# RWKV layer: one masked copy for both heads' grams of a chunk, and the key rates multiplied on ScalarE

## The reference

```python
a = jax.nn.sigmoid(a0 + fa @ w_a2)
kk = (k * k_k).reshape(b, s, RWKV_HEADS, HEAD_DIM).astype(jnp.float32)
kk = kk / jnp.maximum(jnp.linalg.norm(kk, axis=-1, keepdims=True), L2_EPS)
k = k * (1 + (a - 1) * k_a)
def step(state, inp):
    r_t, w_t, k_t, v_t, kk_t, a_t = inp
    sa = jnp.einsum('bhij,bhj->bhi', state, -kk_t)
    state = (state * w_t[:, :, None, :]
             + sa[..., None] * (kk_t * a_t)[:, :, None, :]
             + v_t[..., None] * k_t[:, :, None, :])
    y_t = jnp.einsum('bhij,bhj->bhi', state, r_t)
    return state, y_t
```

## Time and profile before

| | us |
|---|---|
| median of 3 runs | 1768.92 |
| lowest and highest | 1768.81 and 1769.65 |
| the profiled execution, its time | 1768.42 |
| its span, first to last instruction | 1766.6 |

### The profile page before, as it was taken

One profiled execution on the slowest core, in us unless ns is written; L12 is line 12 of the kernel. 1 busy time (PEld: TensorE's weight loads), 2 busy tenths in 40 slices (PEclk: granted clock), 3 DMA queues, 4 the chain that ended last, 5 costly groups with the idle time before them and its releaser, 6 DMA issues.

```text
span 1766.6 us, 22241 instructions
## 1 busy us (share of the span) xinstructions
PE 1739.8 (98%) x9398; PEld 1436.9 (81%) x9398; DVE 845.3 (48%) x1216; ACT 723.7 (41%) x1092; POOL 502.2 (28%) x126
## 2 busy tenths in 40 slices
PE   9999999999999999999999999999999999999998
PEld 8897778888888788888888888877778888888887
DVE  3015467998989864261124443627744411123244
ACT  5244544655555443252222223536652522222222
POOL 2442300000000003424444444243334244444442
PEclk9999999999999999999999999999999999999999
DMA  5432231011111124422222222222222222222221
GB/s 194 167 125 72 79 113 57 28 42 35 28 29 47 37 90 161 143 98 102 99 96 95 96 95 96 104 98 72 72 96 96 85 98 100 102 101 100 96 95 72
DMA packets 57238, 159.46 MB, mean 90 GB/s; under 512 B 3471, under 2 KB 35087, under 8 KB 42548
## 3 DMA queue, kind: packets, MB, share of 16 engines
q1 hardware_dynamic: 45132, 137.64, 22.7%
q10 hardware_dynamic: 12008, 20.40, 3.3%
HBM read 150.41 MB, written 9.19 MB: 90 GB/s over the span
## 4 chain that ended last, share of the span: by engine, by line
PE 89%; DVE 6%; ACT 4%; issue 1%; ACTq 0%; DVEq 0%
PE ps L651 25%; PE ps L653 24%; PE ps L652 24%; PE ps L1123 2%; PE ps L1111 1%; ACT ht_hi L1497 1%; PE ps L1203 1%; PE ps L1165 1%; PE ps L1131 1%; PE ps L1040 1%; DVE ht_lo L2240 1%; PE ps L1155 1%; PE ps L868 1%; PE ps L1175 1%; PE ps L837 1%
## 5 line engine op out<-in xcount | busy, mean ns | idle before, releaser
L642 POOL TENSOR_TENSOR w_lo<-w_raw,w_hi 128x2048 fp32r<-128x2048 f32 (+2 forms) x122 | 502.0, 4120 | 1237.4 <-ACT w_hi L1462 1214.4
L651 PE MATMUL ps<-ht_hi,w_hi 128*128 128x512 f32 (+1 forms) x1312 | 524.6, 400 | 4.8 <-DVE ht_lo L2240 3.2
L653 PE MATMUL ps<-ht_hi,w_lo 128*128 128x512 f32 (+1 forms) x1312 | 499.5, 381 | 0.0
L652 PE MATMUL ps<-ht_lo,w_hi 128*128 128x512 f32 (+1 forms) x1312 | 498.7, 380 | 0.0
L1462 ACT ACTIVATE w_hi<-w_raw 128x2048 fp32r<-128x2048 f32 x125 | 239.2, 1915 | 454.4 <-PE ps L653 400.1
L651 PEld LDWEIGHTS ps<-ht_hi,w_hi 128*128 128x128 f32 x1312 | 247.3, 189 | 64.7 <-issue 19.1
L653 PEld LDWEIGHTS ps<-ht_hi,w_lo 128*128 128x128 f32 x1312 | 246.9, 188 | 48.3
L652 PEld LDWEIGHTS ps<-ht_lo,w_hi 128*128 128x128 f32 x1312 | 247.9, 189 | 39.2 <-issue 1.9
L2836 DVE TENSOR_TENSOR hid_lo<-hidden,hid_hi 128x1024 fp32r<-128x1024 f32 x27 | 129.3, 4788 | 149.1 <-ACT hid_hi L2038 149.1
L651 PE MATMUL ps<-w_hi,hid_hi 128*128 128x512 f32 x432 | 168.4, 390 | 0.0
L653 PE MATMUL ps<-w_hi,hid_lo 128*128 128x512 f32 x432 | 168.3, 390 | 0.0
(11 more groups left out here) (350 smaller groups left out, 2362.2 us busy)
## 6 DMA issues: line engine op xcount, KB each, us to landing
w_raw<-in_wpack SPq DMA_DIRECT2D x113, 1024.0 KB, 4.8
w_raw<-in_wpack SPq DMA_DIRECT2D x26, 512.0 KB, 5.1
x_res<-in_x SPq DMA_DIRECT2D x4, 512.0 KB, 5.6
gate_back<-gate_dram ACTq DMA_DIRECT2D x2, 1024.0 KB, 6.4
gate<-gate_dram ACTq DMA_DIRECT2D x1, 2048.0 KB, 8.3
x_res<-in_x ACTq DMA_DIRECT2D x1, 2048.0 KB, 7.9
bias_skewed_dram<-bias_rows_dram ACTq DMA_DIRECT2D x1, 1792.0 KB, 10.9
gate_dram<-rwkv_out ACTq DMA_DIRECT2D x6, 256.0 KB, 3.4
```

The costliest lines, as they stand in the source:

```text
L642: last = nc.gpsimd.tensor_tensor(Wl[:, slot, cc], raw[:, slot, cc], f32(Wh[:, slot, cc]), ALU.subtract)
L651: mm(dst, wh, ah, start=first, stop=False)
L652: mm(dst, wh, al, start=False, stop=False)
L653: return mm(dst, wl, ah, start=False, stop=last)
```

## The change

A tile `one_less_k_a` (128 x 8) is filled once with 1 - k_a by one small DVE instruction after the constants have landed. ACT gets a new step `rate_factors(c)`: a Copy with a scale per partition that writes `work_t` = iclr * k_a, counted as a third event of `sig_ready` per pair (so the others' counts change from two to three per pair). DVE's `key_scale` loses its TENSOR_SCALAR and computes key * (work_t + (1 - k_a)) in one instruction, behind that third event. The two gram buffers become one tile, laid out as before, and one COPY_PREDICATED per chunk takes both heads, with the mask repeated over the heads. On ACT `rate_factors` stands behind `key_squares(0)` in the first step, and right behind the second sigmoid in `second_step` and in `step(p)` for p = 0 to 5.

```diff
+        OK = fixed("one_less_k_a", [P, PAIRS])
...
-        GM = [r(f"gram{h}", [P, NT, 3, P]) for h in range(2)]
+        GMB = r("gram", [P, 2, NT, 3, P])
+        GM = [GMB[:, h] for h in range(2)]
...
+            def rate_factors(c):
+                w("sig_ready", 3, c, 2)
+                inc(actf(T1[:], Ab[:], ACT.Copy, scale=pcol("k_a", c)), "sig_ready")
...
                 key_squares(0)
+                rate_factors(0)
                 key_root(0)
...
                 sigmoids(1, 1)
+                rate_factors(1)
                 take_half(15)
...
                     sigmoids(c, 1)
+                    rate_factors(c)
                 rhs(a, 2)
...
+            order(v.tensor_scalar(OK[:], PR[:, PC["k_a"]:PC["k_a"] + PAIRS], -1.0, 1.0, ALU.mult, ALU.add))
...
-                w("sig_ready", 2, c, 2)
-                order(v.tensor_scalar(T1[:], Ab[:], -1.0, pcol("k_a", c), ALU.add, ALU.mult))
-                order(v.scalar_tensor_tensor(kk_, T1[:], 1.0, kk_, ALU.add, ALU.mult))
+                w("sig_ready", 3, c, 3)
+                order(v.scalar_tensor_tensor(kk_, T1[:], OK[:, c:c + 1], kk_, ALU.add, ALU.mult))
...
-                for h in range(2):
-                    ins = v.copy_predicated(GM[h][:, t, :, :].rearrange("p a b -> p (a b)"), mask, ps[:, 2 + h, 0:3 * P])
-                inc(ins, "gram_taken")
+                inc(v.copy_predicated(GMB[:, :, t, :, :].rearrange("p h a b -> p h (a b)"),
+                                      mask.unsqueeze(1).to_broadcast([P, 2, 3 * P]), ps[:, 2:4, 0:3 * P]), "gram_taken")
```

More of the change, by code:

```diff
@@ L1049, in key_sums @@
             def key_sums(c):
-                w("sig_ready", 2, c, 1)
+                w("sig_ready", 3, c, 1)
                 w("sq_ready", 1, c, 1)
@@ L2641, in first_step @@
                 for h in range(2):
-                    order(v.memset(GM[h][:], 0.0))
+                    order(v.memset(GM[h], 0.0))
                 dve.wait_ge(sides_in, 16)
```

## The result

The changed kernel takes **1777.41 us** (median of 4 runs, 1777.12 to 1777.57), the kernel before 1769.29 beside it (1768.81 to 1770.22). The ratio is 1.0049, with a 95% interval of 1.0036 to 1.0062: slower by 8.1 us. The forecast was 1768.7, with a range of 1767.0 to 1770.7, and it gave a slowdown of more than 0.2% a chance of 0.06. It was wrong.

What follows compares the result with a forecast made beforehand. PE was taken to bound the kernel, busy 1739.8 of 1766.6 us (98%). The terms +0.62 - 0.51 + 0 - 0.24 - 0.08 = -0.2 us, added to the median of 1768.92, gave 1768.7 us, range 1767.0 to 1770.7.

Steps and rivals of the forecast that it cites:

- the new small instruction: DVE's computing of 1 - k_a, at the beginning of its 85.10 us gap before the first logits: cost nothing.
- The first step of the pipeline: `rate_factors(0)` between ACT's square and table load delays `norm_sq`, so PE waits 2.2 us in place of 1.59: +0.62 us.
- The second step of the pipeline: One DVE TENSOR_SCALAR less ahead of `tinv_t`, for which PE waits 0.56 us at 255.34: -0.51 us.
- Steps 0 to 5: DVE waits for the factors the 0.5 us it no longer computes, and `rhs_sb` moves by 0.61: 0 us on PE.
- The cover of `rhs_sb`: In steps 0 to 5, 0.50 us left between the end of the delayed `rhs_sb` copy and PE's solve.
- The rival of the state chain: ACT's new copy ahead of `rhs_sb` delays the recurrence in six steps: 1773.2 us in full (0.04), 1770.4 in part (0.05).
- The grams: One merged copy of 1.02 us replaces two taking 1.05, shortening PE's six gram waits by 0.04 each: -0.24 us.
- The end of step 5: PE's 0.72 us wait at 597.33 behind DVE's queue shrinks through two gram copies, 0.04 each: -0.08 us.

Runs made afterwards that it cites:

- the tile at home: The changed kernel with all edits, but `one_less_k_a` put in 32 free bytes at the end of `consts`, other addresses as before: 1769.34 us, ratio 1.0002.
- the two with every distance broken: The kernel before with unused bytes ahead of `ht_lo`, `w_raw`, the hidden tiles and `hid_hi`, in two sets of sizes: 1796.39 and 1794.64 us.

## Why the prediction was wrong, and where it was right

**The step that failed** is the first term of the sum, "the new small instruction ... Cost nothing". The instruction costs nothing. The tile that it writes was not looked at: I costed an instruction and not an allocation. The prediction names no place behind 597 us and no rival there, and so the range could not hold the result. In its place the runs showed 8 us: the tile pushes the hidden tiles 64 bytes on, and the pitch of the 1296 matmuls that load them goes from 226.7 to 233.3 ns. The run with 64 unused bytes and the run with the tile at home show from both sides that the address alone makes the difference.

**The first step of the pipeline** was +0.62 by the sum. The wait for `norm_sq` is 2.12 in place of 1.59, +0.53. The timeline of ACT shows the factors at 216.76, and the table load 0.72 behind them:

```profile
216.15 0.71 ACT L1796 ACTIVATE work_x<-rkv,params_sb 128x512 f32<-128x512 f32 x1
216.76 0.71 ACT L1684 ACTIVATE work_t<-iclr,params_sb 128x512 f32<-128x512 f32 x1
217.48 1.28 ACT L1723 ACT_TABLE_LOAD   x1
```

From the start of the square to the table load it is now 217.48 - 216.15 = 1.33 us, and was 217.03 - 216.31 = 0.72. So the insertion costs 0.61 us, as forecast, and the table load waits for the end of what stands ahead of it in both kernels. Some 0.06 come back on the way to `norm_sq`. The matmul that reads it is at 223.01 against 222.61, +0.40, since the changed kernel was ahead by 0.16 when the squares began.

**The second step of the pipeline** was -0.51. The row of the wait for `tinv_t` is gone, but the list shows only waits above 0.15 us. The starts tell more: from the matmul that waits for `tinv` to the one that reads `tinv_t` it was 255.34 - 252.72 = 2.62 us and is 255.31 - 253.14 = 2.17, so 0.45 were won of the 0.51. DVE has the reason:

```profile
252.91 0.75 DVE L2495 SCALAR_TENSOR_TENSOR rkv<-work_t,one_less_k_a,rkv 128x512 f32<-128x512 f32 x1
253.69 0.75 DVE L2583 COPY_PREDICATED inverse<-consts,ps 128x512 f32<-128x512 int32 x1
```

The new instruction takes 0.75 us where the old one took 0.69, and 253.69 - 252.91 = 0.78 stand in place of 253.73 - 252.49 = 1.24. The step was right, with 0.05 less than its price.

**Steps 0 to 5** were 0 on PE, and are, but for less than 0.1 us in the last of them: PE's wait for `tinv` at 566 us is 0.23 to 0.25 us in the three kernels with the factors on ScalarE and 0.16 in the others. DVE waits there as said, but longer. Waits, then the timeline of DVE in step 1:

```profile
DVE rkv L2495 <- ACT work_t L1684: 5.0, 6, 0.8
```

```profile
359.96 0.75 DVE L2495 SCALAR_TENSOR_TENSOR rkv<-work_t,one_less_k_a,rkv 128x512 f32<-128x512 f32 x1 [0.82 <-ACT work_t L1684]
360.75 0.75 DVE L2341 SCALAR_TENSOR_TENSOR rkv<-ps,one_less_mu,gate_tile 128x511 f32<-128x511 f32 x1
```

It is 0.82 us in place of 0.5. The timeline of ACT has the reason:

```profile
358.42 0.68 ACT L1680 ACTIVATE iclr<-ps,params_sb 128x512 f32<-128x512 f32 x1
359.13 0.72 ACT L1684 ACTIVATE work_t<-iclr,params_sb 128x512 f32<-128x512 f32 x1
359.76 0.26 ACT L1804 ACTIVATE rhs_sb<-ps 128x128 f32<-128x128 f32 x1
359.92 0.68 ACT L1583 ACTIVATE gate_tile<-ps,params_sb 128x512 f32<-128x512 f32 x1
```

The factors start 0.71 us behind the sigmoid, where I let them start 0.57 behind it as `rhs_sb` had done. They read what the sigmoid writes, and the line `w("sig_ready", 3, c, 2)` holds them until it has counted, while `rhs_sb` overlapped it. So "no gain and no loss on DVE" was off: set against PE, which is 0.06 us later here, the key scaling starts 0.2 us later than before, and line 2341 behind it 0.1 us later, since it had waited 0.20 anyway. The cover of `rhs_sb` held all the same: it ends at 360.02, the solve starts at 360.42, and it had no wait for ACT in any step. The rival of the state chain did not come.

**The grams** were 1.02 us a copy and -0.24 us. The group of DVE in the changed kernel:

```profile
L2620 DVE COPY_PREDICATED gram<-consts,ps 128x768 f32<-128x768 int32 x32 | 33.3, 1041 | 0.3
```

The mean is 1041 ns, and 1021 where the tile is at home. The six waits went from 0.25 to between 0.22 and 0.24, -0.12 us in all. In the runs with the old addresses they went to 0.21: 0.04 each there, as worked out. By an estimate from the Trainium skill, page "VectorE: DVE Perf Modes", section on the errata of trn2 (120 cycles at 0.96 GHz for each copy from PSUM), the merge would save 0.125 us a chunk; the waits show 0.04, so the measurement decides against it here.

**The end of step 5** was -0.08 and is 0: the wait stays at 0.72.

Through 597 us the sum was -0.2 and the trace has +0.35. The terms as measured do not give that: the matmul at 292.10 in the kernel before is at 292.10 with the change too, and the +0.35 grows behind it. That can't be told from the spread of the profiled executions. The kernel with the hidden tiles 512 bytes on has no edit and no shift in the RWKV stage, and the same two matmuls are at 291.82 and 597.33 in it, so it falls back by 0.29 there. It doesn't bear on the verdict: with the tile at home the ratio is 1.0002 (0.9992 to 1.0011), which is what the forecast said of the edits.

**What stays open.** Why the distance matters was not measured. Beside each of these matmuls runs the load for the next one, and with `hid_hi` alone moved the longest pitches are those during which it is loaded. So the two reads of SBUF side by side are a possible cause, but no run here separates them. How the price comes about where the three matmuls have different distances (the run with `hid_hi` alone, and the two with every distance broken) is open too. Shifts of the hidden tiles between 128 and 256 bytes were not tried, and 32, 256 and 512 each rest on one execution.

## What to carry to other kernels

Ask of every new tile what it pushes, not only what it costs: put a small one in the free tail of another, or last, so that no large one moves. Where matmuls follow each other without a pause, keep every tile that PE loads at a multiple of 256 bytes from the tiles that it streams (the shifts of 0, 256 and 512 were free here), and after an edit compare the number of matmuls in a window that the edit doesn't touch. An edit that wins on an engine with idle time to spare is worth only the few waits of the bound engine that it ends: here 0.45 us once and 0.04 us six times.

## What the runs showed of the hardware

- In the down projections, 128x512 matmuls follow each other after 226.7 ns where all loaded tiles start a multiple of 256 bytes from the streamed ones (shifts of 0, 256 and 512), and after 232.4 to 233.3 on average where they are 32, 64 or 128 off: 2.5 to 2.9% of a stage that PE bounds. Where only some of the tiles are off, the others' matmuls slow down too (229.2 and 232.3). Other engines and DMAs have no part in it (233.3 without any of them at work). A shift of all tiles together by 64 bytes does nothing (1.0000).
- On ScalarE the factors, which wait by a semaphore for the sigmoid ahead of them (0.68 us long), start 0.71 us behind it; the `rhs_sb` copy, which does not need it, started 0.57 behind it and starts 0.63 behind the factors.
- A COPY_PREDICATED over two PSUM banks with a repeated mask takes 1021 to 1041 ns on average for 768 elements, as the line through 384 and 512 elements has it (1.02 us). The two single copies took 1.05 us together, since the second starts before the first has ended.
